# Expert blocks of 32 rows on four column tiles, in place of 64 rows on two, in a one-core encoder trunk

## The reference

```python
t = h.reshape(B * S, D)                                   # 512 tokens, D = 1024
g_idx = argmax(t @ w_rg + b_rg)                           # 1 of 4 groups
top_v, top_i = top_k(expert logits of that group, 2)      # 2 of 4 experts in it
hid = silu(t @ w_gate[e]) * (t @ w_up[e])                 # (tokens, 512), for each expert e
out += combine[:, e] * (hid @ w_down[e])                  # (tokens, 1024)
```

## Time and profile before

| | us |
|---|---|
| median of 3 runs | 668.23 |
| lowest and highest | 665.90, 670.97 |
| the profiled execution, in all | 673.25 |
| its span, first to last instruction | 671.4 |
| granted TensorE clock, mean | 0.967 of full speed |

### The profile page before, as it was taken

How to read it: one execution, slowest core, us unless ns; L and a number is a source line. 1 busy time by engine, 2 the same in 40 slices (tenths; PEclk the granted TensorE clock), 3 DMA queues, 4 the chain that set the end, 5 groups by cost and what they waited for, 6 DMA issues and landing times.

```text
span 671.4 us, 9274 instructions
## 1 busy us (share of the span) xinstructions
PE 611.9 (91%) x3330; PEld 385.3 (57%) x3331; DVE 215.8 (32%) x480; ACT 202.2 (30%) x440; POOL 59.8 (9%) x105
## 2 busy tenths in 40 slices
PE   2899999999999999996889999999999999925995
PEld 2798877878989899953323333333333333304884
DVE  3612264556254442364011010111111110163563
ACT  5532354545444533332000000101010100152674
POOL 0000000000000000002011212121212212110000
PEclk9999999999999999978989999999999999975998
DMA  8743213112211079763999899997998999935001
GB/s 305 186 171 114 74 64 125 63 55 72 64 63 63 1 280 394 298 256 113 362 329 396 329 386 395 361 358 282 397 399 320 392 395 397 408 121 218 33 32 62
DMA packets 76272, 153.34 MB, mean 228 GB/s; under 512 B 7944, under 2 KB 27024, under 8 KB 75984
## 3 DMA queue, kind: packets, MB, share of 16 engines
q1 hardware_dynamic: 72000, 139.24, 56.9%
q0 software_dynamic: 3952, 12.85, 5.1%
q10 hardware_dynamic: 288, 0.81, 0.3%
HBM read 142.66 MB, written 10.23 MB: 228 GB/s over the span
## 4 chain that ended last, share of the span: by engine, by line
PE 80%; DMA 9%; DVE 3%; ACT 3%; issue 2%; SPq 2%; POOLq 0%; ACTq 0%; DVEq 0%; POOL 0%
PE bank L1539 20%; PE bank L1288 12%; PE bank L1289 12%; PE bank L1290 12%; PE bank L1563 10%; DMA ple_gate_raw<-in_w_ple_gate 4%; PE bank L1365 2%; DMA ring_gu<-in_w_up 2%; PE bank L1486 2%; PE bank L1527 2%; SPq L569 2%; PE bank L1338 2%; DMA small<-const_small 1%; PE bank L1379 1%; PE bank L1551 1%
## 5 line engine op out<-in xcount | busy, mean ns | idle before, releaser
L1539 PE MATMUL bank<-ring_gu,rowsT 128*64 128x512 f32 x736 | 166.6, 605 | 5.1 <-issue 4.1
L1539 PEld LDWEIGHTS bank<-ring_gu,rowsT 128*64 128x64 f32 x736 | 51.4, 139 | 104.2 <-issue 103.1
L1563 PE MATMUL bank<-ring_dn,hidT 128*64 128x512 f32 x368 | 84.0, 598 | 1.4 <-DVE hidT L1191 1.4
L857 ACT ACTIVATE silu_g<-bank 128x256 f32<-128x256 f32 x23 | 8.8, 383 | 240.2 <-PE bank L1539 240.2
L1036 DVE TENSOR_TENSOR w_lo<-w_raw,w_hi 128x2048 fp32r<-128x2048 f32 x18 | 41.3, 2293 | 80.3 <-ACT w_hi L722 71.1
L1186 DVE TENSOR_TENSOR hid<-silu_g,bank 128x256 f32<-128x256 f32 x23 | 9.7, 422 | 169.7 <-ACT silu_g L857 169.7
L1288 PE MATMUL bank<-w_hi,hT_hi 128*128 128x256 f32 x192 | 55.9, 291 | 0.0
L1289 PE MATMUL bank<-w_lo,hT_hi 128*128 128x256 f32 x192 | 54.9, 286 | 0.0
L1290 PE MATMUL bank<-w_hi,hT_lo 128*128 128x256 f32 x192 | 54.8, 286 | 0.0
L1288 PE MATMUL bank<-hT_hi,w_hi 128*128 128x512 f32 x128 | 50.8, 397 | 0.0
L1563 PEld LDWEIGHTS bank<-ring_dn,hidT 128*64 128x64 f32 x368 | 24.4, 136 | 44.7 <-issue 44.7
(11 more groups left out here) (208 smaller groups left out, 898.0 us busy)
## 6 DMA issues: line engine op xcount, KB each, us to landing
ring_gu<-in_w_gate SPq DMA_DIRECT2D x32, 1024.0 KB, 13.6
ring_gu<-in_w_up SPq DMA_DIRECT2D x32, 1024.0 KB, 15.1
ring_dn<-in_w_down SPq DMA_DIRECT2D x16, 2048.0 KB, 12.3
w_raw<-in_w_in SPq DMA_DIRECT2D x14, 1024.0 KB, 5.0
w_raw<-in_w_out SPq DMA_DIRECT2D x4, 1024.0 KB, 5.0
ple_gate_raw<-in_w_ple_gate SPq DMA_DIRECT2D x1, 4096.0 KB, 26.0
yg<-y_rows SPq DMA_DIRECT2D x8, 512.0 KB, 7.0
xr<-in_x SPq DMA_DIRECT2D x4, 512.0 KB, 7.5
```

Of the source, the lines that this page charges most:

```text
L1539: last = T.matmul(b_gu[q * BLK:(q + 1) * BLK, :], rowsT[:, k % 4, k // 4, :], ring_gu[s][:, k, :, q * UC:(q + 1) * UC], start=(k == 0), st ...
L1563: last = T.matmul(b_dn[q * BLK:(q + 1) * BLK, :], hidT[:, kf % 2, kf // 2, :], ring_dn[s][:, kf, q * (D // 2):(q + 1) * (D // 2)], start=( ...
```

## The change

Blocks have 32 rows. A token's 1024 values are four rows of 256 in `h2_rows` and `y_rows` (a gathered or scattered tile is 128 partitions of 1 KB in place of 2 KB), and each product is cut into four column tiles of 32 in place of two of 64. A gate/up matmul now covers 256 columns (128 of gate, 128 of up), a down matmul 256. There are two row transposes and one hidden transpose for four and two. `MAX_BLOCKS` goes from 31 to 47, `TABLE` from 34 to 49, the block tables from 32 to 48 entries. Two row buffers take the place of three, and the loops have two blocks in a turn (TensorE had three, the other engines six). Several buffers move in SBUF; since `blk_rows` now lies elsewhere and `ones` too, VectorE waits for the first store into `y_rows` (L640) before it writes `slot_oh`.

```diff
-BLK = 64
+BLK = 32
+NQ = P // BLK
-ROW_BUFS = 3
-GROUP = 6
-PE_GROUP = 3
+ROW_BUFS = 2
+GROUP = 2
+BLOCKS = 48
+QUARTER = D // NQ
+FQ = D_EXPERT // NQ
...
-        rowsT = at("rowsT", 68, [P, 4, 2, BLK])
-        silu_g = at("silu_g", 70, [P, UC])
+        rowsT = at("rowsT", 66, [P, QUARTER // P, NQ, BLK])
+        silu_g = at("silu_g", 67, [P, FQ])
...
-        h2_rows = nc.dram_tensor("h2_rows", [2 * SEQ, HALF], F32, kind="Internal").ap()
-        y_rows = nc.dram_tensor("y_rows", [2 * N_PAIRS + 2, HALF], F32, kind="Internal").ap()
+        h2_rows = nc.dram_tensor("h2_rows", [NQ * SEQ, QUARTER], F32, kind="Internal").ap()
+        y_rows = nc.dram_tensor("y_rows", [NQ * N_PAIRS + NQ, QUARTER], F32, kind="Internal").ap()
...
+                dve.wait_ge(s_ystored, 16)
                 V.tensor_tensor(slot_oh[:], wide(in_blk[:], P), all_pairs(slot_of_row), ALU.is_equal)
...
-                V.tensor_copy(y_blk[buf][:], b_dn[:]).then_inc(y_ready, 1)
+                V.tensor_copy(y_blk[buf][:], b_dn[:, 0:QUARTER]).then_inc(y_ready, 1)
...
-                for j in range(4):
+                for j in range(QUARTER // P):
                     last = T.transpose(b_xT[:, j * P:(j + 1) * P], rows[buf][:, j * P:(j + 1) * P], ident)
...
-                        for q in range(2):
-                            last = T.matmul(b_gu[q * BLK:(q + 1) * BLK, :], rowsT[:, k % 4, k // 4, :],
-                                            ring_gu[s][:, k, :, q * UC:(q + 1) * UC],
+                        for q in range(NQ):
+                            last = T.matmul(b_gu[q * BLK:(q + 1) * BLK, 0:2 * FQ], rowsT[:, k % 2, k // 2, :],
+                                            ring_gu[s][:, k, :, q * FQ:(q + 1) * FQ],
                                             start=(k == 0), stop=(k == KD - 1))
...
-                for j in range(2):
-                    last = T.transpose(b_hT[:, j * P:(j + 1) * P], hid[:, j * P:(j + 1) * P], ident)
-                last.then_inc(hT_done, 1)
+                T.transpose(b_hT[:, 0:P], hid[:], ident).then_inc(hT_done, 1)
...
-                        for q in range(2):
-                            last = T.matmul(b_dn[q * BLK:(q + 1) * BLK, :], hidT[:, kf % 2, kf // 2, :],
-                                            ring_dn[s][:, kf, q * (D // 2):(q + 1) * (D // 2)],
+                        for q in range(NQ):
+                            last = T.matmul(b_dn[q * BLK:(q + 1) * BLK, 0:QUARTER], hidT[:, kf, :],
+                                            ring_dn[s][:, kf, q * QUARTER:(q + 1) * QUARTER],
                                             start=(kf == 0), stop=(kf == D_EXPERT // P - 1))
...
-            over_blocks(pe, total, step, group=PE_GROUP)
+            over_blocks(pe, total, step)
```

## The result

The median goes from 667.2 us (665.9 to 671.0) to 706.7 us (704.0 to 708.3): a ratio of 1.056, 95% interval 1.052 to 1.060. The profiled execution of the changed kernel has a span of 702.0 us, beside 671.4 before; the prediction was 734 us with a range of 702 to 780, so the measured median lies 5 us above the lower end.

What follows compares the result with a forecast made beforehand. TensorE's sequencer, its control code no longer covered by queued matmuls, was to set 8.65 us a block. The stage's 8.3 + 320.1 + 3.7 + 13.8 = 345.9 us against 280.6, plus 0.5 for tables, gave 734 us, range 702 to 780.

Steps and rivals of the forecast that it cites:

- Blocks and groups: Expert stage: 39 blocks for 23; four column tiles run fully together, 0.215 us a group of four matmuls.
- The 0.27 us by the 2.38x: Rival on tile overlap: groups of 0.27 us, 9.5 us a block, 766 us; within partial overlap or clock, chance 0.20.
- The rival at 0.43 us a group: Only two tiles run at a time, TensorE binds: 11.6 us a block, about 845 us; chance 0.04.
- TensorE's own work: Matmul groups, transposes and tile-shape changes of a block: 6.1 us, 238 us over 39 blocks against 266.
- Gate/up to down: First gate/up matmul to first down matmul: 2.37 us of handing on plus 2.7 of control code and start.
- Handing on: Sequencer passes a product's last matmul with 18 waiting: 2.37 us after gate/up's first, 0.86 after down's.
- Down to gate/up: First down matmul to next gate/up: 0.86 us of handing on plus 2.72 of control code, start and loop turn.
- Start and end: Stage's edges: block 0 to 1 8.3 us, a first-visit branch 3.7, the end after last gate/up starts 13.8.
- The sum: Expert stage 345.9 us against 280.6, +65.3; with +0.5 for tables, +65.8 on the span.
- Tables, `ple_gate_raw`, row gathers, weights: Side work: tables +0.5 us, the `ple_gate_raw` load no longer waited for, gathers and weights never late.
- The clock: Forecast case: no fall in the new gaps near 1 and 1.6 us; rival, with partial overlap: it falls, 0.20.
- "Faster", from 6.9 us a block: Rival: control code stays hidden behind queued matmuls, deciding from 6.9 us a block; 646 us, chance 0.06.

Runs made afterwards that it cites:

- a_one_split: Changed kernel, no range checks, one four-register table read a block, two scatters in flight: 664.4 us, ratio 0.989 to before; again 661.3 us, 0.988.
- a_extra: Changed kernel with one more table read and range check in `in_slot`, twice a block: 762.1 us, ratio 1.140 to before.
- a_hoist: Changed kernel with down's two table reads and their checks moved up to gate/up's, nothing removed: 780.9 us, ratio 1.167 to before.
- a_one: Changed kernel, no range checks, one four-register table read a block, one scatter in flight: 677.1 us, ratio 1.011 to before.
- a_split: Changed kernel, no range checks on the table reads, two scatters in flight for one: 673.4 us, ratio 1.004 to before.
- a_three: Changed kernel, one unchecked read a block, two scatters in flight, three row buffers, TensorE's loop unrolled three times, the others six: 915.0 us, ratio 1.366 to before.

## Why the prediction was right

The mechanism, its sign and its place were right: two idle stretches a block with the releaser "issue", a clock of 1.00, no wait for weights. The size was 29 us too large on the stage (65.3 for 36.0) and 26 on the median, almost to the edge of the range. By the steps:

- **Blocks and groups.** 39 blocks, as forecast. Four tiles run fully together: the 64 matmuls of a gate/up take 3.66 us, 16 groups of 0.216 and the change of shape; forecast 0.215. The Trainium skill (TensorEngine Tiling (Array Packing), Theoretical Speedup) has up to 4x for four such tiles, and the trace agrees as far as the pair of the earlier trace rows can be the measure: half its 0.43 us; no run has one tile alone. The 0.27 us by the 2.38x of the Trainium skill (TensorE: Matmul & The Clock Gate, Part 3) does not show. The rival at 0.43 us a group would be 10.32 + 0.91 = 11.2 us a block, not the 11.6 written, which changes no chance. TensorE's own work, forecast 6.1 us a block, is 6.08 in the fastest blocks of `a_one_split`.
- **Gate/up to down, forecast 2.37 + 2.7 = 5.07 us, measured 4.54.** Handing on is right: 2.46 us in the block at 445.95, with 16 of 64 matmuls still waiting (forecast 18). The control code was mis-sized. These are the two reads ahead of down, before and then after (ns, start us):

```profile
L1513 PEldq TENSOR_LOAD <-blk_loads x1: 441/441/441, 451.3 to 451.3; - x1
```

```profile
L1517 PEldq TENSOR_LOAD <-blk_loads x1: 318/318/318, 448.7 to 448.7; - x1
...
L1519 PEldq COMPARE_BRANCH  x2: 71/122/172, 448.4 to 450.0; - x2
```

  In before the read starts 0.8 us behind the branch (450.5); after, 0.3 us behind it (448.4 to 448.7). In between stand only the row transposes. The likely reason is that they must find room in a full queue: four there, where two matmuls start every 0.43 us, and two here, where four start in half of that. By this reading, which no run isolates, the 2.6 us of the earlier trace rows were partly the wait for the queue, not control code; and the reads themselves were shorter here (318 for 441 ns). From the branch to the first down matmul (448.41 to 450.35) it was 1.94 us, not 2.7.
- **Down to gate/up, forecast 0.86 + 2.72 = 3.58 us, measured 3.13.** Control was right, some 2.65. Handing on was not: down's branch came 0.47 us after its first matmul, in the third group, with 21 or 22 of 32 matmuls waiting, where I had put 14. The 14 of the earlier trace rows were not what the queue holds; down has 16 matmuls, two had started, and there were no more to queue. Two windows of the kernel after, gate/up's matmuls up to its branch and down's up to its own:

```profile
445.90:448.40 2.50, 2.45 (x48) 1.57 (x52) 1.00 1.04 318
```

```profile
450.30:450.81 0.51, 0.46 (x10) 0.31 (x13) 1.00 1.01 369
```

  So 64 - 48 = 16 waited in the one and 32 - 10 = 22, or one fewer, in the other: the number is not a constant, and I don't know what sets it.
- **Start and end.** Block 0 to 1: 9.1 us for 8.3, its gate/up 6.46 for 5.2. Blocks 1 and 2 together: 24.2 us for the 21.0 that two blocks and the long branch made; there are two long branches, 1.56 us at 325.4 and 3.50 at 329.4, and behind the idle time the gate/up products of these blocks take 5.45 and 5.89 us for 3.66, a loss of clock that the sum had only for block 0. The end, 14.4 for 13.8. Together +4.6 us; 35 blocks at 7.67 for 8.65 make -34.
- **The sum.** From the first gate/up to the last copy of `y_blk`, 312.4 to 629.0, the stage takes 316.6 us against 280.6: +36.0, forecast +65.3. It starts 3.8 us earlier than in the profile of before and what follows it is 1.6 shorter, which leaves +30.6 on the span. The medians differ by 39.4, since the profiled execution of before lies above its median and that of after below: against the spans the forecast is 35 us too large, not 26.
- **Tables, `ple_gate_raw`, row gathers, weights.** No wait for any of them in the stage, as forecast. The scatter was taken as a little too short: `y_rows` lands after 6.7 us in the median, 9.3 at most, for 6.2; GpSimd waits for it in 3 blocks and VectorE in 10 (18.9 us), near the edge at 7.67 us a block already.
- **The clock.** It did not fall in the steady part, as the forecast case had it; `a_extra` and `a_hoist` show that little was missing: with 0.65 us more of gap ahead of gate/up it falls in 5 of 33 blocks, with 1.4 more in 26. At the 8.65 us a block of the forecast, with about 0.5 us more in each gap than came, it might thus have fallen in some.
- **"Faster", from 6.9 us a block.** The mark was a little high: `a_one`, at 6.90, is 1% slower, `a_split`, at 6.83, 0.4% slower, and `a_one_split`, at 6.45, 1.2% faster.

What stays open: why 16 matmuls wait in the one place and 21 or 22 in the other, why the blocks 7, 15 and 23 of `a_split` are those whose gather is late, and why in the kernel after the gaps follow a pattern that repeats every eight blocks (from the last down matmul to gate/up 0.64 to 1.71 us, around the mean of 1.20).

## What to carry to other kernels

Smaller tiles that run together let matmuls start faster and so shrink the time that the waiting ones cover: here from 3.9 us for 18 to about 0.9 us for 16, while TensorE's own work in the stage goes from 266 to some 237 us (39 blocks of 6.08). Before cutting work into shorter instructions, set the control code between two runs of them against what is queued there, place by place, and pay for it first (one read for several registers, no range checks, no order that fills one place and empties the other). With that paid, the shorter blocks were the faster ones here, by 1.2% (some 0.7% against before with the same single read), where they had been 5.6% slower. A queue's depth is read where the instructions outnumber it, and a stretch of control code where the queue in front of it isn't full.

## What the runs showed of the hardware

- Control code of TensorE's sequencer, each by the trace: a TENSOR_LOAD of one register 0.31 us in the median (0.30 to 0.58, before and after), one of four registers 0.54 (`a_one_split`), a range check 0.15 and 0.02 and gaps beside. A read with its check lengthened the two gaps of `a_extra` by 0.46 and 0.65 us.
- An idle TensorE can pay twice. From block 6 on, gate/up took 3.66 us in every block of after, where the time from the last down matmul to the first of gate/up (the hidden transpose included) is at most 1.71 us. It was longer in 5 of 33 blocks of `a_extra`, behind 2.15 to 2.32 us, and in 26 of `a_hoist`, behind 2.3 to 3.2; but gate/up took 3.66 us also behind 2.36 us in the one and 2.76 in the other, so that time alone doesn't decide it. The 74 us of `a_hoist` are more clock than gap.
- A loop body too long for what is kept fetched cost 250 us in `a_three`, the lower clock included, far more than its unrolling could save; the instruction queue's packets on the page (24 and 136) show it at once.
